# Two passes over the sixth expert tile, with the end of the query stage beside it

## The chip, the cores and the metric

The kernel runs on one core of one Trainium2 chip. The metric is the device time of one execution in microseconds (us); shown are the median of three runs and one profiled execution.

## What is computed

The reference is one step of a streaming trunk of two layers over 640 tokens of width 1024 (512 of a prompt, 8 streams of 16). Each layer mixes tokens (a Mamba-2 scan and an RG-LRU side by side) and then adds the output of retrieved experts. The experts are what the change moves:

```
def peer(h, wq, k1, k2, u, v):                       # per token, 8 heads
    q = (h @ wq).reshape(T, 8, 256)
    s1, s2 = q[..., :128] @ k1.T, q[..., 128:] @ k2.T   # 128 keys each
    v1, i1 = top_k(s1, 16); v2, i2 = top_k(s2, 16)
    sv, si = top_k(v1[..., :, None] + v2[..., None, :], 16)   # of 256 sums
    e = i1[si // 16] * 128 + i2[si % 16]             # 16 experts of 16384
    g = softmax(sv)
    act = gelu(h . u[e]) * g                         # 128 experts a token
    return sum(act * v[e])
...
x = x + g1 * token_mixer(rmsnorm(x) * (1 + sc1) + sh1)
x = x + g2 * peer(rmsnorm(x) * (1 + sc2) + sh2)
```

All of it is fp32. A token takes 128 experts, each a row of u and a row of v (8 KB together), and no two tokens share their choice.

## The kernel before

**Tiles and regions.** The 640 tokens of a layer are five tiles of 128, so there are ten expert tiles, 0 to 9; 0 to 4 are of layer 0. Token mixing and the query stage run over regions: region 0 is tiles 0 to 2 and region 1 is tiles 3 and 4, both of layer 0; regions 2 (tiles 5 to 7) and 3 (tiles 8 and 9) are their like in layer 1. "The sixth tile" is tile 5, the first of layer 1.

**Units and pairs.** An expert tile is 128 units. A unit is one indirect transfer of 128 rows of 8 KB from the table (1.049 MB) into one of the 8 slots of `ring`: four picks of each of the 32 tokens of one block. Two units make a pair, so a tile has 64 pairs, here written (tile, pair). For a pair VectorE multiplies and sums the u halves against `hrow` (`dots`, L1902), ScalarE makes gelu, weight and diagonal of both units (`diagonals`, L1366 to L1376), and TensorE in the next pair multiplies the v halves with the diagonals into PSUM (`values`, L1008) and so frees the two slots; GpSimd (L600) may then start the transfers of the pair four pairs on. `hrow` holds the tokens of one block, turned into rows by TensorE (`turn_h`, L1030) and copied by ScalarE (`h_row`, L1395) in two halves.

**Passes.** A tile in one pass goes through its four blocks once, 32 units each, for all 8 heads. Tile 0 goes in two passes: the four blocks with heads 0 to 3 (16 units each), then the four blocks with heads 4 to 7. Its gathers can therefore start when four heads are chosen. PSUM keeps the sums of the blocks between the passes; `hrow` is changed eight times a tile and not four.

**Steps.** The mixing of a region is a list of numbered steps, in stages: N1 (norm, 12), X (13), S (15 or 19), Z (8), LX (9), LRU (8), M (merge, 33), OUT and the second norm (18), Q (query, 22). A step with a projection takes one 0.524 MB weight tile, loaded by the SP queue (L447) into four slots, four projections ahead. In the Q stage steps Q0 to Q15 project the queries; from Q4 to Q19 VectorE finds the 16 best keys on each side, head by head, for all tiles of the region (`best_keys`), and for the region's first tile also its experts (`sum_up`, `look_up`, `put`) and gates. For the other tiles of a region the experts are chosen later from the kept best keys: a choice of 28 pieces, one per pair (`choice`), at a place given by `choice_at`. When a tile's experts are known VectorE raises `ready`, and the SP queue spreads the picks (`spread`, L533: 16 small transfers from `picked` to `units`), for which GpSimd's first gather of the tile (or of the pass) waits.

**The order.** `plan` writes out by hand one list of entries; an entry is at most one pair and some steps. Every engine walks this list in order. `window(pairs, steps, at, till)` lays steps beside pairs evenly by their weights in `SHARE`, from the pair number `at` to `till`. The plan says which step lies beside which pair; worked out from it:

```
what                                    before               pairs
region 2: N1, X, S                      (3,9)  to (3,30)     22
region 2: Z, LX                         (3,31) to (3,46)     16
region 2: LRU, M                        (3,47) to (4,23)     41
region 2: OUT, second norm              (4,24) to (4,33)     10
region 2: Q0 to Q3                      (4,34) to (4,38)      5
region 2: Q4 to Q13                     (4,39) to (4,51)     13
region 2: Q14 to Q21                    (4,52) to (4,58)      7
choice of tile 6, 28 pieces             (4,59) to (5,23)
region 3: N1, X0 to X9                  (5,9)  to (5,23)     15
region 3: X10 to LX0                    (5,24) to (5,53)     30
region 3: LX1 to LX7                    (5,54) to (5,63)     10
tile 0 and region 0: Q14 to Q21         (0,1)  to (0,15)     15
tile 0 and region 1: N1, X0 to X9       (0,16) to (0,29)     14
tile 0 and region 1: X10 to LX0         (0,30) to (0,58)     29
tile 0 and region 1: LX1 to LX4         (0,59) to (0,63)      5
choice of tile 1, 28 pieces             (0,30) to (0,58)
```

Regions 1 and 3 have the same steps, of the same sizes.

Of the kernel before, what the change touches and what calls it, by code (L numbers as in the profile page):

```python
# [26 lines left out]
BLOCKS = P // BLOCK  # L27
# [85 lines left out]
def around(s, p):  # L113


    if s == TILES_E:
        return BLOCKS * s - 1, None, p
    e, block, quad, place = segment(s, 2 * p)
    i = 2 * p // length(s)
    past = BLOCKS * s + block - 1 if i >= BLOCKS * (passes(s) - 1) and BLOCKS * s + block else None  # L120
    if s == 0 and i == BLOCKS:
        past = None
    after = (s, (block + 1) % BLOCKS) if i + 1 < BLOCKS * passes(s) else (s + 1, 0) if s + 1 < TILES_E else None
    return past, after, place // 2


def plan():
# [22 lines left out]
    def pairs_of(*tiles):  # L150
        return [(s, p) for s in tiles for p in range(PAIRS)]
# [6 lines left out]
    window(first[-14:], [(EARLY, i - BASE[EARLY]["X"]) for i in range(BASE[EARLY]["X"])], 1, 13)  # L158
    window(pairs_of(3, 4), steps_of(2), 9, 122)
    window(pairs_of(5, 6, 7), steps_of(3), 9, 180)  # L160
    window(pairs_of(8), [(REGIONS + t, i) for t in range(3) for i in range(FINAL)], 9, 60)
# [59 lines left out]
def choice_at(t):  # L221


    return PAIRS * (t - 1) + {1: 30, 4: -12, 6: -5}.get(t, 8)

# [9 lines left out]
def passes(s):  # L235
    return 1 if s else 2

# [6 lines left out]
def segment(s, u):  # L244

    i, place = divmod(u, length(s))
    h, block = divmod(i, BLOCKS)
    return (i if s == 0 else 4 * BLOCKS // 2 + BLOCKS * (s - 1) + i), block, h * length(s) + place, place


def spreads(s):

    return BLOCKS * BLOCKS * (s + 2)

# [16 lines left out]
def build(nc, a):  # L271
    ctx = ExitStack()
    with ctx:
# [164 lines left out]
        with nc.Block() as block:  # L438
            @block.sync
            def _(sp):  # L440
# [84 lines left out]
                def spread(s, h):  # L525

                    sp.wait_ge(E["ready"], s + h + 1 if s == 0 else s + 2)
                    if s >= 2:
                        sp.wait_ge(E["wgt"], (s - 1) * UNITS)
                    c = slice(h * length(s), (h + 1) * length(s)) if s == 0 else slice(0, QUADS)  # L530
                    for block in range(BLOCKS):
                        for r in range(BLOCKS):
                            sp.dma_start(units[r * BLOCK:(r + 1) * BLOCK, s % 2, block, :, c],  # L533
                                         picked[block * BLOCK:(block + 1) * BLOCK, s % 2, r, :, c]).then_inc(E["spread"], 16)
# [3 lines left out]
                for e, steps in PLAN:  # L538
                    while n < min(taken + SLOTS, REGIONS * LOADS):
                        next(ahead)  # L540
                    t, place = choice(*e) if e else (None, None)
                    if place == 28:
                        spread(t, 0)
                    for r, i in steps:
                        if r < REGIONS:
                            taken += loads_in(r, i)
                            if r == 0 and i == BASE[0]["Q"] + 13:
                                spread(0, 0)
                            if i == BASE[r]["Q"] + 21:
                                spread(TILE0[r], passes(TILE0[r]) - 1)  # L550
# [4 lines left out]
            def _(pool):  # L555
# [33 lines left out]
                for s in range(TILES_E):  # L589
                    for u in range(UNITS):  # L590
                        if u == 0:
                            pool.wait_ge(E["spread"], 16 * (spreads(s) if s else BLOCKS * BLOCKS))
                        elif s == 0 and u == UNITS // 2:
                            pool.wait_ge(E["spread"], 16 * spreads(0))
                        unit = s * UNITS + u
# [9 lines left out]
            def _(pe):  # L605
# [390 lines left out]
                def values(pair):  # L996
# [3 lines left out]
                    for u in (2 * p, 2 * p + 1):  # L1000
                        unit = s * UNITS + u
                        n = unit % RING
                        e, block, quad, place = segment(s, u)
                        if place == 0 and BLOCKS * s + block >= 2 and (s or quad):
                            pe.wait_ge(E["osb"], BLOCKS * s + block - 1)
# [42 lines left out]
                def pair(s, p):  # L1048
# [3 lines left out]
                    past, after, place = around(s, p)  # L1052
                    if past is not None and place == TURN_OUT[s > 0]:
                        turn_out(past)
                    for half in range(2):
                        if after and place == TURN_H[s > 0][half]:
                            turn_h(*after, half)
# [11 lines left out]
            def _(act):  # L1069
# [328 lines left out]
                def pair(s, p):  # L1398
                    if s < TILES_E:
                        diagonals(s, p)  # L1400
                    past, after, place = around(s, p)
                    if past is not None and place == TAKE_OUT[s > 0]:
                        take_out(past)
                    for half in range(2):
                        if after and place == COPY_H[s > 0][half]:
                            h_row(s, p, half)
# [28 lines left out]
            def _(dve):  # L1435
# [396 lines left out]
                def q_stage(r, i):  # L1832
# [6 lines left out]
                    if 8 <= i < 21 and i % 4 == 0:  # L1839
                        m = (i - 8) // 4  # L1840
                        dve.wait_ge(S["q_ex_out"], at("q_ex_out", r, m))
                        gates(gate_of(s, 2 * m), den[:, 2 * m:2 * m + 2])
                        if m == 3 or r == 0 and m == 1:
                            dve.sem_inc(E["ready"], 1)
# [82 lines left out]
                def pair(s, p):  # L1927
                    if s < TILES_E:
                        dots(s, p)
                    past, _, place = around(s, p)  # L1930
                    if past is not None and place == ADD[s > 0]:
                        residual(past)
# [114 lines left out]
```

## Time and profile before

| | us |
|---|---|
| median of 3 runs (4547.33 to 4551.07) | 4549.44 |
| the profiled execution | 4542.65 |
| its span, first to last instruction | 4540.9 |

The profiled execution lies 1.75 us over its span and 6.79 us under the median of the runs. Of the span TensorE is busy 71%, VectorE 62%, ScalarE 33% and GpSimd 32%; the sixteen DMA engines moved 1610.83 MB, 1342.26 of them in the gathers. A busy share says little here, since every engine walks the same list; what counts is which resource is full in which stretch. GB/s by slice shows where the transfers, which cannot be fewer, are held up. The trace shows pairs by their L1902 instructions: four for a pair, two of them a multiply with sum and two the read of the sum.

### The profile page before, as it was taken

The numbers are of one execution on the slowest core, as the hardware profiler recorded it, in microseconds if no ns is written. First come the engines' busy times: TensorE is split into PE (matmuls) and PEld (weight loads), VectorE is DVE, ScalarE is ACT, GpSimd is POOL, SyncE is SP. The second block draws the span as 40 slices with busy tenths as digits, with TensorE's granted clock in tenths as the row PEclk, the third lists the DMA queues.
The fourth block names the chain that finished last, engine by engine and source line by source line (L and its number), as shares of the span: only waits on it lengthen the run. The fifth ranks groups of instructions, "written<-read, shape, count | busy, mean of one in ns | idle before, by whom it ended". The sixth has DMA issues, their size and how long they took to land. (4 is left out here: it accounts for less than half of the span.)

```text
span 4540.9 us, 60485 instructions
## 1 busy us (share of the span) xinstructions
PE 3202.5 (71%) x22002; PEld 1894.3 (42%) x22002; DVE 2825.0 (62%) x6601; ACT 1484.8 (33%) x4684; POOL 1454.2 (32%) x1298
## 2 busy tenths in 40 slices
PE   7899994777687675489999855776777764444443
PEld 4455552445454442245555423454554442121111
DVE  2422048796864579876744798756854588675454
ACT  2224011543622223354722323534522222232222
POOL 0000003443333343334333323443333334444332
PEclk9999996878898886599999976878888786555555
DMA  8333327999999999989999979999999999999998
GB/s 335 137 146 102 100 81 315 385 373 388 417 417 418 416 405 382 393 340 351 390 386 392 378 283 372 416 387 397 418 418 419 418 411 364 421 419 422 421 421 335
DMA packets 279860, 1610.83 MB, mean 355 GB/s; under 512 B 56410, under 2 KB 61328, under 8 KB 112524
## 3 DMA queue, kind: packets, MB, share of 16 engines
q0 software_dynamic: 184320, 1342.26, 72.4%
q1 hardware_dynamic: 75280, 256.81, 15.1%
q10 hardware_dynamic: 19964, 7.91, 0.6%
q8 instruction: 174, 2.85, 0.3%
q14 instruction: 122, 1.00, 0.1%
HBM read 1597.63 MB, written 7.91 MB: 354 GB/s over the span
## 5 line engine op out<-in xcount | busy, mean ns | idle before, releaser
L600 POOL DMA_INDIRECT ring<-in_peer_uv,units x1280 | 1451.0, 1134 | 3051.8 <-PE psum L1008 2136.4
L1902 DVE SCALAR_TENSOR_TENSOR ring<-ring,hrow 128x1024 f32<-128x1024 f32 x1280 | 1537.6, 1223 | 829.6 <-DMA ring<-in_peer_uv,units 793.9
L1008 PE MATMUL psum<-ring,diag 128*32 128x256 f32 x10240 | 920.3, 491 | 1156.9 <-ACT diag L1376 1153.0
L613 PE MATMUL psum<-hT,wslot 128*128 128x384 f32 (+1 forms) x4224 | 1264.0, 456 | 7.7 <-ACT region L1267 3.1
L1008 PEld LDWEIGHTS psum<-ring,diag 128*32 128x32 f32 x10240 | 320.3, 130 | 1669.5 <-ACT diag L1376 1352.1
L613 PEld LDWEIGHTS psum<-hT,wslot 128*128 128x128 f32 x4224 | 832.6, 201 | 434.3 <-issue 93.4
L1366 ACT ACTIVATE gel<-hid 128x2 f32<-128x2 f32 x640 | 129.1, 202 | 1823.9 <-DVE ring L1902 1767.8
L613 PE MATMUL psum<-region,wslot 128*128 128x384 f32 (+1 forms) x1536 | 458.9, 455 | 3.5 <-ACT region L1267 1.9
L613 PEld LDWEIGHTS psum<-region,wslot 128*128 128x128 f32 x1536 | 302.3, 201 | 154.6 <-issue 31.9
L1376 ACT ACTIVATE diag<-pick,wgt 128x32 f32<-128x32 f32 x1280 | 331.8, 306 | 0.0
L1370 ACT ACTIVATE wgt<-gel,units 128x1 f32<-128x1 f32 x1280 | 307.3, 287 | 20.9
L1522 DVE SCALAR_TENSOR_TENSOR region<-region,vec 128x384 f32<-128x384 f32 (+1 forms) x144 | 80.9, 562 | 182.1 <-ACT region L1142 170.4
L1030 PE MATMUL psum<-ident,hT 128*32 128x128 f32 x2816 | 133.8, 351 | 40.7 <-ACT hrow L1395 30.4
L1030 PEld LDWEIGHTS psum<-ident,hT 128*32 128x32 f32 x2816 | 111.4, 145 | 75.4 <-ACT hrow L1395 28.2
L1280 ACT ACTIVATE region<-psum 128x384 f32<-128x384 f32 (+1 forms) x64 | 27.6, 431 | 305.5 <-PE psum L613 305.5
L1902 DVE DVE_READ_ACCUMULATOR ring<-ring,hrow 128x1 f32 x1280 | 104.7, 82 | 0.0
L1735 DVE SCALAR_TENSOR_TENSOR region<-region,psum 128x384 f32<-128x384 f32 (+1 forms) x32 | 15.5, 486 | 126.3 <-PE psum L613 126.2
L1659 DVE SCALAR_TENSOR_TENSOR region<-region,psum 128x384 f32<-128x384 f32 (+1 forms) x32 | 15.6, 486 | 113.8 <-ACT region L1224 113.7
L1729 DVE SCALAR_TENSOR_TENSOR region<-region,psum 128x384 f32<-128x384 f32 (+1 forms) x32 | 15.5, 485 | 110.2 <-PE psum L613 71.4
L1366 ACT ACT_TABLE_LOAD x65 | 83.4, 1283 | 1.8 <-issue 0.6
L645 PE MATMUL psum<-ring,cT 128*32 128x512 f32 x384 | 47.6, 614 | 31.0 <-DMA ring<-in_w_modt 15.6
L1315 ACT ACTIVATE region<-psum 128x384 f32<-128x384 f32 (+1 forms) x64 | 27.2, 426 | 114.8 <-PE psum L613 114.6
(247 smaller groups left out, 2810.6 us busy)
## 6 DMA issues: line engine op xcount, KB each, us to landing
wslot<-in_w_tiles SPq DMA_DIRECT2D x360, 512.0 KB
ring<-in_w_modt SPq DMA_DIRECT2D x24, 2048.0 KB, 8.9
ring<-in_peer_uv,units POOLq DMA_INDIRECT x1280
wslot<-in_w_gate SPq DMA_DIRECT2D x32, 128.0 KB
region<-in_states_t SPq DMA_DIRECT2D x16, 256.0 KB, 23.3
region<-in_states_n SPq DMA_DIRECT2D x16, 256.0 KB, 8.2
out_new_ssd_sample<-region ACTq DMA_DIRECT2D x16, 256.0 KB, 30.9
xT<-in_x_t SPq DMA_DIRECT2D x1, 2560.0 KB, 8.9
```

What stands on the lines that cost most here:

```text
L600: pool.indirect_dma_start(ring[:, n, :], None, table, bass.IndirectOffsetOnAxis(ap=units[:, s % 2, block, 0, quad:quad + 1].bitcast(U32), ...
L613: last = pe.matmul(out, wslot[:, n % SLOTS, k * P:(k + 1) * P], src(k), start=k == 0, stop=k == KT - 1)
L645: last = pe.matmul(bank(5)[32 * q:32 * q + 32, :], cT[:, 2 * q + kk, :], w, start=kk == 0, stop=kk == 1)
L1008: last = pe.matmul(psum[c * BLOCK:(c + 1) * BLOCK, block % 2, block // 2 * 256:(block // 2 + 1) * 256], diag[:, n, :], ring[:, n, D + c * ...
L1030: last = pe.matmul(out[c * BLOCK:(c + 1) * BLOCK, :], v, ident[:], start=True, stop=True)
L1280: act.activation(lay.gates[:, q, :], bank(3 + 2 * q)[:, 0:lay.N], ACT.Tanh, scale=0.5).then_inc(S["mg"], 1)
L1315: act.activation(lay.qT[:, j % 2, q, :], bank(3 + q)[:, 0:lay.N], ACT.Copy).then_inc(S["q_taken"], 1)
L1366: act.activation(gel[:, v], hid[:, v], ACT.Gelu_apprx_tanh).then_inc(E["gelu"], 1)
L1370: act.activation(wgt[:, c:c + 1], gel[:, c:c + 1], ACT.Copy, scale=units[:, s % 2, block, 1, quad + u:quad + u + 1])\
L1376: act.activation(diag[:, pick % RING, :], pick32[:], ACT.Copy, scale=wgt[:, pick % 16:pick % 16 + 1])\
L1522: st(dve.scalar_tensor_tensor(y, x[:, k:k + NY], w(k), y, ALU.mult, ALU.add))
L1902: dve.scalar_tensor_tensor(out=ring[:, n, 0:D], in0=ring[:, n, 0:D], scalar=1.0, in1=hrow[:, e % 2, :], op0=ALU.mult, op1=ALU.mult, accum_ ...
```

## The change

Tile 5 goes in two passes, as tile 0 does (`passes`), and the functions that had tile 0 written into them (`segment`, `spreads`, `around`, `spread`, the waits of GpSimd and TensorE, the places of the hand-overs in a block of 8 pairs) go by `passes(s)`. The plan's two windows from tile 3 to tile 7 become three: region 2 up to Q13 beside the first 124 pairs of tiles 3 and 4, its last eight steps Q14 to Q21 beside 16 pairs (four of tile 4, twelve of tile 5), and region 3 from pair 12 of tile 5 on. The choice of tile 6, which needs the best keys of all eight heads, moves from pair -5 to pair 30 of tile 5 (`choice_at`).

```
what                                    after                pairs
region 2: N1, X, S                      (3,9)  to (3,32)     24
region 2: Z, LX                         (3,33) to (3,49)     17
region 2: LRU, M                        (3,50) to (4,29)     44
region 2: OUT, second norm              (4,30) to (4,40)     11
region 2: Q0 to Q3                      (4,41) to (4,45)      5
region 2: Q4 to Q13                     (4,46) to (4,60)     15
region 2: Q14 to Q21                    (4,61) to (5,11)     15
region 3: N1, X0 to X9                  (5,12) to (5,26)     15
region 3: X10 to LX0                    (5,27) to (5,56)     30
region 3: LX1 to LX5                    (5,57) to (5,63)      7
choice of tile 6, 28 pieces             (5,30) to (5,58)
```

Region 3 ends beside the same pair of tile 7 as before. The spread of tile 5's first four heads lies at Q13, pair (4,59), and that of the other four at Q21, pair (5,9).

```diff
--- before.py
+++ after.py
@@ -117,9 +117,7 @@
         return BLOCKS * s - 1, None, p
     e, block, quad, place = segment(s, 2 * p)
     i = 2 * p // length(s)
-    past = BLOCKS * s + block - 1 if i >= BLOCKS * (passes(s) - 1) and BLOCKS * s + block else None
-    if s == 0 and i == BLOCKS:
-        past = None
+    past = BLOCKS * s + block - 1 if i > BLOCKS * (passes(s) - 1) or s and i == 0 else None
     after = (s, (block + 1) % BLOCKS) if i + 1 < BLOCKS * passes(s) else (s + 1, 0) if s + 1 < TILES_E else None
     return past, after, place // 2
 
@@ -156,8 +154,10 @@
     first = fresh + pairs_of(1, 2)
     window(first[:-14], steps_of(1), 0, 64 - 28 + 125)
     window(first[-14:], [(EARLY, i - BASE[EARLY]["X"]) for i in range(BASE[EARLY]["X"])], 1, 13)
-    window(pairs_of(3, 4), steps_of(2), 9, 122)
-    window(pairs_of(5, 6, 7), steps_of(3), 9, 180)
+    half = BASE[2]["Q"] + 14
+    window(pairs_of(3, 4)[:124], steps_of(2)[:half], 9, 124)
+    window(pairs_of(3, 4)[124:] + pairs_of(5)[:12], steps_of(2)[half:], 0, 14)
+    window(pairs_of(5)[12:] + pairs_of(6, 7), steps_of(3), 0, 168)
     window(pairs_of(8), [(REGIONS + t, i) for t in range(3) for i in range(FINAL)], 9, 60)
     window(pairs_of(9), [(REGIONS + 3, i) for i in range(FINAL)], 9, 60)
     for p in range(9):
@@ -221,7 +221,7 @@
 def choice_at(t):
 
 
-    return PAIRS * (t - 1) + {1: 30, 4: -12, 6: -5}.get(t, 8)
+    return PAIRS * (t - 1) + {1: 30, 4: -12, 6: 30}.get(t, 8)
 
 
 def choice(s, p):
@@ -233,7 +233,8 @@
 
 
 def passes(s):
-    return 1 if s else 2
+
+    return 2 if s in (0, 5) else 1
 
 
 def length(s):
@@ -245,12 +246,12 @@
 
     i, place = divmod(u, length(s))
     h, block = divmod(i, BLOCKS)
-    return (i if s == 0 else 4 * BLOCKS // 2 + BLOCKS * (s - 1) + i), block, h * length(s) + place, place
+    return BLOCKS * sum(passes(t) for t in range(s)) + i, block, h * length(s) + place, place
 
 
 def spreads(s):
 
-    return BLOCKS * BLOCKS * (s + 2)
+    return BLOCKS * BLOCKS * sum(passes(t) for t in range(s + 1))
 
 
 def state_loads(l, i):
@@ -524,10 +525,10 @@
 
                 def spread(s, h):
 
-                    sp.wait_ge(E["ready"], s + h + 1 if s == 0 else s + 2)
+                    sp.wait_ge(E["ready"], sum(passes(t) for t in range(s)) + h + 1)
                     if s >= 2:
                         sp.wait_ge(E["wgt"], (s - 1) * UNITS)
-                    c = slice(h * length(s), (h + 1) * length(s)) if s == 0 else slice(0, QUADS)
+                    c = slice(h * length(s), (h + 1) * length(s))
                     for block in range(BLOCKS):
                         for r in range(BLOCKS):
                             sp.dma_start(units[r * BLOCK:(r + 1) * BLOCK, s % 2, block, :, c],
@@ -544,8 +545,8 @@
                     for r, i in steps:
                         if r < REGIONS:
                             taken += loads_in(r, i)
-                            if r == 0 and i == BASE[0]["Q"] + 13:
-                                spread(0, 0)
+                            if passes(TILE0[r]) == 2 and i == BASE[r]["Q"] + 13:
+                                spread(TILE0[r], 0)
                             if i == BASE[r]["Q"] + 21:
                                 spread(TILE0[r], passes(TILE0[r]) - 1)
                 for _ in ahead:
@@ -589,9 +590,9 @@
                 for s in range(TILES_E):
                     for u in range(UNITS):
                         if u == 0:
-                            pool.wait_ge(E["spread"], 16 * (spreads(s) if s else BLOCKS * BLOCKS))
-                        elif s == 0 and u == UNITS // 2:
-                            pool.wait_ge(E["spread"], 16 * spreads(0))
+                            pool.wait_ge(E["spread"], 16 * (spreads(s) - BLOCKS * BLOCKS * (passes(s) - 1)))
+                        elif passes(s) == 2 and u == UNITS // 2:
+                            pool.wait_ge(E["spread"], 16 * spreads(s))
                         unit = s * UNITS + u
                         n = unit % RING
                         _, block, quad, _ = segment(s, u)
@@ -1001,7 +1002,7 @@
                         unit = s * UNITS + u
                         n = unit % RING
                         e, block, quad, place = segment(s, u)
-                        if place == 0 and BLOCKS * s + block >= 2 and (s or quad):
+                        if place == 0 and BLOCKS * s + block >= 2 and (quad or block < 2 or passes(s) == 1):
                             pe.wait_ge(E["osb"], BLOCKS * s + block - 1)
                         pe.wait_ge(E["diag"], unit + 1)
                         for c in range(BLOCKS):
@@ -1050,10 +1051,10 @@
                     if 0 <= n < TILES_E * PAIRS:
                         values(n)
                     past, after, place = around(s, p)
-                    if past is not None and place == TURN_OUT[s > 0]:
+                    if past is not None and place == TURN_OUT[passes(s) == 1]:
                         turn_out(past)
                     for half in range(2):
-                        if after and place == TURN_H[s > 0][half]:
+                        if after and place == TURN_H[passes(s) == 1][half]:
                             turn_h(*after, half)
 
                 pe.wait_ge(consts, CONSTS)
@@ -1399,10 +1400,10 @@
                     if s < TILES_E:
                         diagonals(s, p)
                     past, after, place = around(s, p)
-                    if past is not None and place == TAKE_OUT[s > 0]:
+                    if past is not None and place == TAKE_OUT[passes(s) == 1]:
                         take_out(past)
                     for half in range(2):
-                        if after and place == COPY_H[s > 0][half]:
+                        if after and place == COPY_H[passes(s) == 1][half]:
                             h_row(s, p, half)
                     t, place = choice(s, p)
                     if place == 26:
@@ -1840,7 +1841,7 @@
                         m = (i - 8) // 4
                         dve.wait_ge(S["q_ex_out"], at("q_ex_out", r, m))
                         gates(gate_of(s, 2 * m), den[:, 2 * m:2 * m + 2])
-                        if m == 3 or r == 0 and m == 1:
+                        if m == 3 or passes(s) == 2 and m == 1:
                             dve.sem_inc(E["ready"], 1)
                     if 4 <= i < 20:
                         j = (i - 4) // 2
@@ -1928,7 +1929,7 @@
                     if s < TILES_E:
                         dots(s, p)
                     past, _, place = around(s, p)
-                    if past is not None and place == ADD[s > 0]:
+                    if past is not None and place == ADD[passes(s) == 1]:
                         residual(past)
                     t, place = choice(s, p)
                     if t and place < 24:
```

## Rows read from the trace of the kernel before

**Rows 1.** The page's 40 slices: clock granted to TensorE, transfer rate

```profile
PEclk9999996878898886599999976878888786555555
GB/s 335 137 146 102 100 81 315 385 373 388 417 417 418 416 405 382 393 340 351 390 386 392 378 283 372 416 387 397 418 418 419 418 411 364 421 419 422 421 421 335
```

**Rows 2.** Windows, region 2 beside tiles 3 and 4; busy us by engine

```profile
core 0: us, PE busy (x) PEld busy (x) DVE busy (x) ACT busy (x) POOL busy (x), PEclk, DMA share, GB/s
1909.70:2250.50 340.80, 313.14 (x1906) 174.84 (x1906) 238.74 (x419) 186.19 (x449) 122.50 (x96) 0.94 0.90 351
2250.50:2460.00 209.50, 207.44 (x1116) 111.81 (x1114) 92.84 (x165) 55.74 (x197) 75.80 (x61) 1.00 0.98 391
2460.00:2529.20 69.20, 61.94 (x384) 33.13 (x384) 34.76 (x59) 22.28 (x68) 25.32 (x23) 0.96 0.98 386
2529.20:2554.10 24.90, 23.03 (x121) 12.12 (x118) 12.91 (x24) 9.01 (x33) 9.49 (x8) 0.90 0.97 374
2554.10:2659.60 105.50, 85.62 (x518) 50.20 (x516) 96.41 (x371) 24.29 (x78) 28.37 (x29) 0.92 0.92 353
2659.60:2724.70 65.10, 26.76 (x202) 14.56 (x202) 61.07 (x236) 15.45 (x46) 13.78 (x14) 0.68 0.70 253
```

**Rows 3.** Waits from 2554.1 to 2724.7 us: us, times, longest

```profile
POOL ring L600 <- PE psum L1008: 112.1, 21, 9.8
ACT gel L1366 <- DVE ring L1902: 67.9, 18, 13.1
```

**Rows 4.** Windows, same columns: choice of tile 6, region 3, tile 6

```profile
2724.70:2793.50 68.80, 31.50 (x310) 12.75 (x310) 59.96 (x146) 17.98 (x79) 30.18 (x29) 0.57 0.93 374
2793.50:2883.30 89.80, 70.16 (x463) 49.61 (x462) 78.85 (x185) 47.42 (x180) 31.25 (x30) 0.81 0.97 393
2883.30:3072.20 188.90, 134.36 (x1233) 82.26 (x1231) 117.89 (x191) 70.46 (x213) 80.54 (x60) 0.80 1.00 399
3072.20:3135.30 63.10, 44.35 (x356) 30.10 (x356) 40.24 (x81) 26.22 (x113) 24.03 (x21) 0.85 0.97 379
3135.30:3513.70 378.40, 273.13 (x1995) 185.45 (x1994) 236.43 (x522) 141.91 (x435) 144.85 (x128) 0.85 1.02 418
```

**Rows 5.** Windows, same columns: tile 0 from its second pair, tile 1

```profile
716.30:804.00 87.70, 47.91 (x439) 25.25 (x432) 78.96 (x264) 25.50 (x89) 32.32 (x29) 0.70 0.93 380
804.00:889.60 85.60, 67.18 (x537) 48.44 (x529) 60.04 (x130) 44.22 (x173) 33.95 (x30) 0.88 0.98 392
889.60:1078.50 188.90, 134.24 (x1284) 83.39 (x1281) 157.22 (x321) 72.61 (x215) 76.07 (x58) 0.78 0.97 386
1078.50:1117.80 39.30, 28.51 (x233) 20.80 (x231) 20.64 (x42) 15.39 (x59) 10.95 (x10) 0.85 0.94 352
1117.80:1497.00 379.20, 276.58 (x2039) 188.38 (x2042) 243.68 (x541) 147.52 (x460) 139.17 (x128) 0.85 1.02 418
```

**Rows 6.** Timeline of VectorE around pair (4,46), beside which no step lies

```profile
2615.95 1.23 DVE L1902 SCALAR_TENSOR_TENSOR ring<-ring,hrow 128x1024 f32<-128x1024 f32 x1
...
2618.25 1.22 DVE L1902 SCALAR_TENSOR_TENSOR ring<-ring,hrow 128x1024 f32<-128x1024 f32 x1
```

**Rows 7.** Windows of L1902 alone: four instructions are a pair

```profile
2724.70:2793.50 68.80, 33.71 (x59) 0.57 0.93 374
```

**Rows 8.** Groups of TensorE in the merge stage, 2250.5 to 2460.0 us

```profile
L613 PE MATMUL psum<-hT,wslot 128*128 128x384 f32 x260 | 88.1, 492 | 0.0
...
L1008 PE MATMUL psum<-ring,diag 128*32 128x256 f32 x496 | 33.2, 385 | 1.9 <-ACT diag L1376 1.8
```

**Rows 9.** Timelines of the SP queue at the spreads of tiles 0 and 5

```profile
692.03 10.33 SPq L533 DMA_DIRECT2D units<-picked  x16
...
796.95 10.92 SPq L533 DMA_DIRECT2D units<-picked  x16
...
2722.38 11.30 SPq L533 DMA_DIRECT2D units<-picked  x16
```

**Rows 10.** Waits of the SP queue from 889.6 to 1078.5 us

```profile
SPq L533 <- DVEq L1953: 5.4, 1, 5.4
```

## The prediction

> **What bounds the kernel now.** I first read the 40 slices, 113.5 us each, for the transfer rate. It stands at 416 to 422 GB/s where nothing but gathers and a few weights run, and falls below that in three places after the gathers have begun [rows 1]. Bytes can't be saved (the change moves the same picks and weights), so 418 GB/s, the rate of tiles 1 and 6 [rows 4, 5], is the floor, and the question is how much time the transfers are held up. At 418 GB/s a pair (2.097 MB) is 5.02 us and a weight tile (0.524 MB) 1.25 us.
>
> Then I cut the stretch from pair (3,9) to the end of tile 6 at the borders of the plan's stages, by counting four L1902 instructions to a pair as in [rows 7] (59 for 14 pairs; some records are missing), and read the windows. Time lost against the floor is a window's length times (1 - rate/418). N1 to LRU of region 2 lose 54.6 us, M 13.5, OUT 5.3, Q0 to Q3 2.6, Q4 to Q13 16.4 and Q14 to Q21 25.7 [rows 2]; the first half of tile 6's choice 7.2, region 3 beside tile 5 5.4 + 8.6 + 5.9, tile 6 nothing [rows 4]. That is 145 us in all.
>
> The reader is to see that the cause changes on the way. Up to OUT TensorE is the full one: busy 207.4 of 209.5 us in M at a granted clock of 1.00, while VectorE is busy 92.8. In Q4 to Q21 it is VectorE: 96.4 of 105.5 and 61.1 of 65.1 us, while TensorE falls to 26.8 of 65.1 us and the rate to 253 GB/s [rows 2]. The chain of that stretch stands in the waits: ScalarE's gelu waits 67.9 us for VectorE's products, so diagonals and freed slots come late, and GpSimd waits 112.1 of 170.6 us before it may start the next gather [rows 3]. There VectorE's picking of keys sets the time, and each pair that is laid beside it gets its gathers almost free: pair (4,46), with no step beside it, passes in 2.30 us, the two products alone [rows 6], against 5.02 us of transfer.
>
> **The change part by part.** It removes no work and adds little. It moves pairs: counting from the two tables of the plan, N1 to LRU get 4 pairs more (48 to 52), M 2, OUT 1, Q4 to Q13 2, Q14 to Q21 8 (7 to 15); the 14 pairs with the first half of tile 6's choice vanish as a stretch of their own, and region 3 beside tile 5 has 3 fewer (55 to 52). The sum is zero, as it must be.
>
> *Seven pairs into N1 to OUT.* Here TensorE's projections set the time. A projection instruction of 384 columns takes 88.1/260 = 0.34 us, sixteen a step, 5.4 us; the eight small products of a unit, two units a pair, take 33.2/496 x 16 = 1.07 us [rows 8]. So an added pair costs no less than its 2.30 us on VectorE [rows 6] in order, and no more than 5.02 us of transfer: 16.1 to 35.1 us for seven. The idle transfer time there (54.6, 13.5, 5.3) exceeds what each of the three stretches gets (20.1, 10.0, 5.0), so I take a value near the low end: +18.
>
> *Two pairs into Q4 to Q13.* VectorE-bound, 2.30 us each: +4.6 (up to 10.0).
>
> *Eight pairs into Q14 to Q21.* The trace holds this very stretch once: tile 0 has Q14 to Q21 of region 0, with as many tiles in the region, beside 15 pairs in two passes, and takes 87.7 us at 380 GB/s [rows 5]. Before, it is 65.1 us: +22.6. By eight bare pairs it would be +18.4, with all eight at transfer speed +40.2. Tile 0 includes what two passes add: twice the hand-overs of `hrow` and a second spread.
>
> *The 14 pairs of the choice.* Their stretch is gone: -68.8 [rows 4].
>
> *Region 3 beside tile 5.* Before, 55 pairs from N1 on take 89.8 + 188.9 + 63.1 = 341.8 us [rows 4]. After, 52 pairs hold the steps up to LX5 and all 28 pieces of the choice, with S and Z. Again tile 0 has it: region 1 from N1 to LX4 with the 28 pieces of tile 1 beside X10 to LX0, 48 pairs in 85.6 + 188.9 + 39.3 = 313.8 us [rows 5]. Four more pairs are 9.2 to 20.1 us; most here run at transfer speed, so 16. One more weight tile is 1.3. That is 331.1: -10.7 (-17.5 to -6.6).
>
> *Tiles 6 and 7.* Two steps (LX6, LX7) are owed at the end of tile 5, 2.5 us of weights at most. Tile 1, which also begins that much behind, takes 379.2 us against tile 6's 378.4 [rows 4, 5]. I take +2. From tile 8 on nothing changes.
>
> *The queues.* SP gets one batch of spreads more, and its pieces are half as long. A half batch takes 10.33 and 10.92 us to issue, a full one 11.30 [rows 9], so +10 us on SP. Weights queued behind it are those of region 3, four ahead and not due while Q14 to Q21 run, which cost nothing; without that cover it is +10. The spread of tile 6 moves from X9 to LX2 and can hold SP while it waits for VectorE, 5.4 us in tile 0 [rows 10]; LX3's weights are loaded ahead, and tile 0's window has the same wait inside. "DMA: Bandwidth & Descriptors" of the Trainium skill (Specifications) puts line rate at pieces of 512 B and more, which speaks against pieces of 64 B in place of 128; the rows show that SP's issue sets the price and not the size, so by rule or by row nothing is added.
>
> Sum: 18 + 4.6 + 22.6 - 68.8 - 10.7 + 2 = -32.3 us. The profiled execution of 4542.65 us (span 4540.9 and 1.75 around it) becomes 4510.4; the median of the runs lies 6.79 above it, so 4517.
>
> **The rivals.**
>
> *The seven pairs are not hidden* (chance 0.15). Region 2 loses time in stalls as well as on TensorE, and an added pair's transfer may fall outside them: +35 in place of +18, a sum of -15, 4534 us. For it speaks the M stage at 391 GB/s, only 7% under the floor [rows 2]; against it the 54.6 us lost before M.
>
> *The first gather of tile 5 comes late* (0.06). `ready` comes with Q12 beside (4,57); the spread then takes 10.3 us to issue plus its landing, and GpSimd wants the picks once (4,60) is through, after three pairs at 2.3 and Q13's part of VectorE, some 13 us. The ring holds eight landed units in this stretch, so the loss stays under 10 us: 4527.
>
> *The choice beside S and Z makes it slower* (0.09). Fourteen pieces cost VectorE 59.96 - 33.71 = 26.3 us [rows 4, 7], so 28 cost 52.5. In S and Z each step waits for VectorE's part of an earlier one. If all 52.5 us land on region 3's own pace (188.9 us for X10 to LX0 without a piece [rows 4]), that stretch is 241 and not 193, and the sum is +16: 4565. It ends slower once over 41 of the 52.5 us show. For it: VectorE would be busy 117.9 + 52.5 of 188.9 us, 90%. Against it: tile 0 does the same steps with 28 pieces, at VectorE 157.2 busy, in the same 188.9 us with one pair less [rows 4, 5].
>
> *Transfers are at their limit anyway* (0.04). If the mean rate over the kernel were the limit, spreading pairs would move nothing: 4549, no change. For it: 1610.83 MB over the span are a mean of 355 GB/s. Against it: tile 6 holds 418 for 378 us [rows 4], and the slices reach 422 [rows 1]. "DMA: Bandwidth & Descriptors" of the Trainium skill (Specifications) gives a limit of about 358 GB/s from HBM for one core; by that rule this rival would hold. The trace disagrees by 60 GB/s; the Trainium skill's page adds that single-core runs reach 425.
>
> **How the numbers follow.** The forecast itself has 0.66, with its own bounds: 16.1 + 4.6 + 18.4 - 68.8 - 17.5 = -47, to about -16, where half of what the first rival adds is left open. The range reaches from about -50, a little under the sum of the low bounds, to -5, the sum of the high ones with tile 0's row kept for Q14 to Q21 (35.1 + 10.0 + 22.6 - 68.8 - 6.6 + 2.5): 4499 to 4544. About 9 us (0.2%) is what a measurement tells from no change. Faster: 0.66, two thirds of the first rival and of the late gather, 0.80. Same: the rest of these two, the limit and a touch of the choice, 0.12. Slower: 0.08.
>
> **What would show it.** Right: the window from Q14 to Q21 runs at about 380 GB/s and lasts near 88 us; pair (5,12) starts near 2770 us (1909.7 + 619.5 + 18 + 24.9 + 110.1 + 87.7; pair (5,9) starts at 2793.5 before) and tile 6 near 3101 (before 3135.3); slice 24, the one from 2611 us on (283 GB/s), rises above 340. The first rival shows as N1 to OUT lasting over 650 us; the late gather as GpSimd waiting for `units<-picked` a second time; the choice as VectorE over 90% busy and a rate under 370 GB/s beside S and Z. The prediction would be wrong above all if tile 0's rows, taken with region 0 and 1, do not carry over to tile 5.

## The result and the profile after

The changed kernel takes 4518.92 us (median of 4 runs, 4512.28 to 4523.05) against 4548.39 for the kernel before in the same set: a ratio of 0.9936, 95% interval 0.9924 to 0.9949. A second set, beside other kernels, gave 4520.79 us and 0.9946 (0.9932 to 0.996). The forecast was 4517. The profiled execution took 4512.28 us, 30.4 less than the one of before.

The transfer rate of the changed kernel by slice answers to [rows 1]:

```profile
GB/s 333 135 155 98 103 80 303 382 374 407 418 418 419 419 404 383 418 321 363 397 411 405 409 334 362 403 365 394 418 417 419 418 403 367 421 420 422 421 421 330
```

The slice that stood at 283 GB/s stands at 334, and five of the six before it are higher too; the three behind it (372, 416 and 387 before) are lower. The windows below go by the stages of the plan after: N1 to LRU, M, OUT, Q0 to Q3, Q4 to Q13, Q14 to Q21 with the two bare pairs behind it (pairs with no step beside them), region 3 in three parts beside tile 5, and tile 6. They answer to [rows 2] and [rows 4].

```profile
1903.60:2254.50 350.90, 323.43 (x2006) 179.10 (x2006) 248.39 (x436) 188.28 (x468) 130.04 (x104) 0.92 0.91 361
2254.50:2469.00 214.50, 211.59 (x1185) 113.91 (x1187) 97.77 (x174) 58.39 (x208) 83.89 (x65) 0.99 1.01 408
2469.00:2537.10 68.10, 61.18 (x362) 32.35 (x354) 39.04 (x66) 22.73 (x72) 27.16 (x24) 0.98 1.01 418
2537.10:2563.30 26.20, 25.45 (x158) 13.23 (x148) 12.08 (x21) 8.72 (x31) 9.70 (x8) 0.85 0.95 371
2563.30:2676.40 113.10, 88.08 (x537) 51.00 (x530) 101.88 (x384) 27.03 (x92) 33.23 (x30) 0.89 0.90 348
2676.40:2764.70 88.30, 42.04 (x385) 21.94 (x388) 79.92 (x268) 25.17 (x88) 30.36 (x29) 0.68 0.89 352
2764.70:2854.80 90.10, 75.34 (x579) 52.96 (x572) 62.84 (x136) 46.77 (x185) 39.65 (x33) 0.84 0.98 396
2854.80:3055.50 200.70, 139.77 (x1365) 87.01 (x1363) 159.16 (x322) 72.61 (x216) 69.15 (x60) 0.79 0.96 380
3055.50:3101.30 45.80, 34.39 (x258) 24.22 (x262) 29.14 (x60) 23.23 (x87) 12.77 (x12) 0.80 0.93 359
3101.30:3481.30 380.00, 272.87 (x2038) 185.88 (x2032) 241.08 (x533) 145.18 (x451) 152.80 (x130) 0.86 1.02 418
```

The reader is to see two things. M and OUT went from 391 and 386 GB/s to 408 and 418: three more pairs were put there, and the two stretches together became 3.9 us longer (282.6 for 278.7) where three pairs' transfers at the floor are 15 us. The granted clock did not bring this: it is 0.99 and 0.98 in the two, after 1.00 and 0.96 [rows 2]. And the query stage is still VectorE's: busy 79.9 of 88.3 us in Q14 to Q21, at 352 GB/s. Its ScalarE and GpSimd still wait as in [rows 3], but over 201 us and 30 pairs, no longer over 171 and 20 (waits from 2563.3 to 2764.7 us):

```profile
POOL ring L601 <- PE psum L1009: 130.6, 28, 12.4
ACT gel L1367 <- DVE ring L1903: 106.0, 24, 12.6
```

One number serves for all that follows: the time from pair (3,9), where the two plans part, to the first pair of tile 8, where they have met again. It was 1967.7 us before (1909.7 to 3877.4) and is 1942.1 (1903.6 to 3845.7) in the first profile of the changed kernel, 1937.0 in the second.

### The profile page after: what moved, and what is told of

Same layout as the page of the kernel before. It is cut to its first block and busy times, and to the rows that moved or that the text cites. A ratio compares the mean times of both kernels' runs of the same rounds, so it can differ in the third digit from the quotient of the medians.

```text
span 4510.5 us, 61035 instructions
## 1 busy us (share of the span) xinstructions
PE 3210.7 (71%) x22258; PEld 1901.3 (42%) x22258; DVE 2827.8 (63%) x6601; ACT 1486.8 (33%) x4690; POOL 1458.4 (32%) x1298
## 5 line engine op out<-in xcount | busy, mean ns | idle before, releaser
L1031 PE MATMUL psum<-ident,hT 128*32 128x128 f32 x3072 | 148.3, 352 | 73.6 <-ACT hrow L1396 55.9
L1031 PEld LDWEIGHTS psum<-ident,hT 128*32 128x32 f32 x3072 | 122.0, 145 | 112.5 <-issue 63.1
L1281 ACT ACTIVATE region<-psum 128x384 f32<-128x384 f32 (+1 forms) x64 | 27.6, 432 | 307.1 <-PE psum L614 307.0
L1104 ACT ACTIVATE region<-psum 128x512 f32<-128x512 f32 x24 | 14.3, 597 | 153.7 <-PE psum L654 141.8
```

The costliest lines, as they stand in the source:

```text
L1031: last = pe.matmul(out[c * BLOCK:(c + 1) * BLOCK, :], v, ident[:], start=True, stop=True)
L1281: act.activation(lay.gates[:, q, :], bank(3 + 2 * q)[:, 0:lay.N], ACT.Tanh, scale=0.5).then_inc(S["mg"], 1)
```

## Experiments

Ratios are to the kernel before, run on the same chip, with 95% intervals. "The stretch" is from (3,9) to tile 8, in each one's profile.

**1. The two passes alone.** Everything of the change but the windows and the choice's place. The two lines added at the end make the SP queue wait until the first spread of tile 5 has landed before it issues the second.

```diff
-    half = BASE[2]["Q"] + 14
...
+    window(pairs_of(3, 4), steps_of(2), 9, 122)
+    window(pairs_of(5, 6, 7), steps_of(3), 9, 180)
...
-    return PAIRS * (t - 1) + {1: 30, 4: -12, 6: 30}.get(t, 8)
+    return PAIRS * (t - 1) + {1: 30, 4: -12, 6: -5}.get(t, 8)
...
+                    if s and h:
+                        sp.wait_ge(E["spread"], 16 * (spreads(s) - BLOCKS * BLOCKS))
```

> Tile 5 goes in two passes, but the plan and the place of tile 6's choice stay as before (the SP queue also waits for the first spread before it issues the second). Theory A (the gain is in where pairs lie: beside steps that VectorE or TensorE sets a pair costs 2.0 to 2.3 us, in a stretch at the transfer rate 5): the passes alone bring nothing and cost four more hand-overs and half a spread, which lie under transfers: within 5 us of before, 4545 to 4555. Theory B (the gain comes from gathers of tile 5 that may start early): 4517 to 4535. Theory C (the hand-overs every 8 pairs cost, and the change won in spite of them): over 4555.

Measured: 4552.25 us, ratio 1.0014 (1.0001 to 1.0026); the stretch takes 1966.9 us, 0.8 less than before. Of the 6 us between the medians none is in the stretch, so the passes by themselves bring nothing and cost next to nothing. Theory A's range held, and theories B and C fall. One part did move: region 3's N1 to X9, with the pieces of the choice beside them, took 102.6 us where it took 89.8 [rows 4]; other parts of the stretch were shorter.

```profile
2803.00:2905.60 102.60, 77.03 (x560) 55.16 (x557) 78.32 (x184) 48.00 (x181) 33.52 (x30) 0.79 0.93 368
```

**2. More pairs beside the query stage, without the rest.** The kernel before with heavier weights for Q4 to Q17 of region 2.

```diff
+    if r == 2 and BASE[r]["Q"] + 4 <= i < BASE[r]["Q"] + 18:
+        return 35
     return SHARE[max((BASE[r][name], name) for name in SHARE if BASE[r][name] <= i)[1]]
```

> The kernel before with one pass, but the weights of Q4 to Q17 in region 2 raised from 24 to 35 (6 for none of them): Q4 to Q21 get 6 pairs more (26 in place of 20), all taken from N1 to OUT. Theory A: N1 to OUT loses 6 pairs at the 2.0 us that an added pair cost there in the changed kernel (-12), Q4 to Q21 gains 6 at 2.3 (+14): +2, 4545 to 4555, no change. Theory D (what pays is to relieve the stretch in which VectorE is full, wherever the pairs come from): 6 pairs at 5 us out, at 2.3 in: -16, 4533.

Measured: 4551.83 us, ratio 1.0009 (0.9998 to 1.002); the stretch 1967.5 us. Its windows are N1 to OUT (83 pairs, 89 before), Q4 to Q13 (17 pairs, 13 before) and Q14 to Q21 (8 pairs; 6 before, 62.8 us, without the bare pair of 2.3 us that [rows 2] has in its 65.1):

```profile
1914.20:2520.90 606.70, 572.89 (x3308) 316.59 (x3307) 352.15 (x616) 254.90 (x680) 207.71 (x167) 0.97 0.92 356
2545.50:2663.10 117.60, 91.89 (x597) 53.01 (x596) 106.66 (x392) 28.82 (x99) 38.82 (x36) 0.90 0.96 377
2663.10:2730.60 67.50, 31.74 (x234) 17.13 (x234) 63.47 (x242) 16.96 (x56) 21.11 (x19) 0.70 0.86 328
```

The transfers of the query stage are much better fed (377 and 328 GB/s for 353 and 253), and nothing is won: the query stage is 16.8 us longer for its six pairs (185.1 for 105.5 + 62.8), 2.8 each, and N1 to OUT is 12.8 us shorter for its six, 2.1 each, and sank to 356 GB/s (369 over the same stages before). A high rate in one stage is no gain where the pairs come out of another stage in which they were as cheap. Theory D falls.

**3. The choice at pair 12 and not 30.**

```diff
-    return PAIRS * (t - 1) + {1: 30, 4: -12, 6: 30}.get(t, 8)
+    return PAIRS * (t - 1) + {1: 30, 4: -12, 6: 12}.get(t, 8)
```

> The changed kernel with the choice of tile 6 at pair 12 of tile 5 and not 30, so its 28 pieces lie beside N1, X and the first steps of S. Theory E (the 11.9 us that X10 to LX0 got longer are the pieces beside S and Z): that stretch falls from 200.7 to 189 to 194 us, N1 to X9 rises by at most 3: 4509 to 4515. Theory F (it is the variation of the stalls there, not the pieces): X10 to LX0 stays at 195 to 205, total 4515 to 4523.

Measured: 4527.19 us, ratio 0.9954 (0.9937 to 0.9971); the stretch 1944.7 us.

```profile
2773.60:2883.00 109.40, 79.07 (x600) 54.94 (x592) 90.55 (x227) 47.70 (x189) 39.49 (x35) 0.80 0.91 359
2883.00:3071.80 188.80, 136.92 (x1358) 85.67 (x1358) 130.58 (x236) 72.79 (x215) 75.10 (x60) 0.78 0.97 374
```

X10 to LX0 fell from 200.7 to 188.8 us as theory E expected, but N1 to X9 rose from 90.1 to 109.4, where at most 3 were expected. The sum of the two is 7.4 us worse, and the total lies above the ranges of both theories. The place at pair 30 looks the better one: the stretch is 3 to 8 us shorter with it in the two profiles of the changed kernel (1942.1 and 1937.0), though the intervals of the ratios overlap. It would be so for a reason that the forecast did not have.

**4. Without the pieces.** Left out are the 24 working pieces of tile 6's choice, so that tile 6 gathers by the picks that tile 4 left behind.

```diff
-                    if t and place < 24:
+                    if t and t != 6 and place < 24:
```

> The changed kernel without the 24 working pieces of tile 6's choice; left out is the choice of tile 6's experts, so tile 6 gathers rows of picks that tile 4 left in the buffer. It prices the choice where it now lies. Theory E: X10 to LX0 falls by 8 to 15 us, 4504 to 4511. Theory F: by under 4 us, 4515 to 4523. Were all 52 us of VectorE's work on the path, 4467.

Measured: 4503.52 us, ratio 0.9905 (0.9886 to 0.9924); the stretch 1922.2 us, 14.8 to 19.9 less than in the two profiles of the changed kernel. X10 to LX0:

```profile
2862.50:3048.10 185.60, 134.70 (x1361) 84.63 (x1360) 118.66 (x194) 74.51 (x219) 75.40 (x59) 0.81 1.00 398
```

That is 185.6 against 200.7 and 195.3: VectorE has 40 us less to do there (118.7 for 159.2), and leaving them out shortens it by 10 to 15. Theory E holds, with a total just under its 4504 to 4511, and the rival of the forecast in which over 41 us would show is refuted by size.

**5. The changed kernel again.**

> The changed kernel once more, for the spread between executions and beside the next three on one chip. The 6 us by which its first profile was ahead at pair (3,9), before anything that the change touches, should be chance: (3,9) between 1900 and 1915 us; total 4512 to 4524, ratio to before 0.993 to 0.995.

Measured: 4520.79 us, ratio 0.9946 (0.9932 to 0.996). Its pair (3,9) starts at 1907.4 us, after 1903.6 in the first profile. In the thirteen profiles of this study it starts between 1903.6 and 1919.1 us, though no plan differs before it: that is how far executions differ by chance, and six of the 30 us between the first two profiles are of this kind.

**6. A narrow second window.** Four pairs of tile 5 in place of twelve (and the wait of experiment 1).

```diff
-    window(pairs_of(3, 4)[124:] + pairs_of(5)[:12], steps_of(2)[half:], 0, 14)
-    window(pairs_of(5)[12:] + pairs_of(6, 7), steps_of(3), 0, 168)
+    window(pairs_of(3, 4)[124:] + pairs_of(5)[:4], steps_of(2)[half:], 0, 6)
+    window(pairs_of(5)[4:] + pairs_of(6, 7), steps_of(3), 0, 176)
```

> The changed kernel with the second window over 4 pairs of tile 5 and not 12: Q14 to Q21 beside 7 pairs or so in place of 15, region 3 from pair (5,4). Theory A: eight pairs go from a stretch where one costs 2.3 us to stretches at 380 to 418 GB/s where one costs 4 to 5: +14 to +22 on the changed kernel, 4532 to 4541. Theory B (the early gathers and the choice's new place are what pays): within 4 us of the changed kernel, 4515 to 4523.

Measured: 4518.96 us, ratio 0.9944 (0.9929 to 0.9959); the stretch 1937.7 us: no loss, where 14 to 22 us were expected. Its windows are Q14 to Q21 with two bare pairs (8 pairs, from (4,60)), then region 3 to the end of tile 5:

```profile
2684.00:2751.20 67.20, 29.05 (x197) 16.26 (x199) 62.63 (x235) 15.56 (x46) 14.14 (x14) 0.70 0.69 254
2751.20:3112.30 361.10, 267.00 (x2443) 175.94 (x2436) 277.78 (x567) 158.45 (x548) 153.21 (x122) 0.83 0.99 398
```

Eight pairs (60 for 52) cost 361.1 - 336.6 = 24.5 us beside region 3, 3.1 each and not 4 to 5 (3.5 by the second profile of the changed kernel, 332.8 us), and region 3 also got further by them. The seven fewer beside Q14 to Q21 saved 88.3 - 67.2 = 21.1, 3.0 each, and the eighth came out of Q4 to Q13 (110.8 us for 113.1). The prices are nearly equal, so the width does not matter here. This order has one wait that the changed kernel has not: GpSimd stands 10.3 us for tile 6's picks; what it costs was not taken apart. Theory A had the right kind of price and the wrong one for region 3; theory B's number came true without its reason, which experiments 1 and 10 exclude.

**7. A wide second window.** The same with 24 pairs of tile 5 and 156 for region 3, in two sets.

```diff
+    window(pairs_of(3, 4)[124:] + pairs_of(5)[:24], steps_of(2)[half:], 0, 26)
+    window(pairs_of(5)[24:] + pairs_of(6, 7), steps_of(3), 0, 156)
```

> The second window over 24 pairs of tile 5: Q14 to Q21 beside 27 pairs, region 3 from (5,24), so that the 28 pieces lie beside N1, X and S. Theory A: Q14 to Q21 reaches the transfer floor (27 pairs, 136 to 140 us), so most of the 12 pairs cost 4 to 5 us there too and what region 3 gives back is 12 pairs at about the same: -6 to +2, 4512 to 4521. Theory D (relieving VectorE pays on): -26, 4493. From the run with the choice at 12 a further cost is seen: pieces beside N1 and X cost up to 19 us, which would put it at 4525 to 4540.

> The kernel with the second window over 24 pairs of tile 5 once more, with more rounds, against the changed kernel's ratio of 0.9936 and 0.9946: if its first 0.9928 was no chance, 0.992 to 0.994 again and a profile of 1930 to 1937 us from (3,9) to (8,0) (1942.1 and 1937.0 in the two profiles of the changed kernel).

Measured: 4509.86 us, ratio 0.9928 (0.9911 to 0.9945), and 4510.08 us, ratio 0.9917 (0.9903 to 0.993); the stretch 1934.2 and 1934.5 us. It is the fastest full version found, 11 us ahead of the changed kernel by the medians of one set (4509.86 and 4520.79) and under theory A's range of 4512 to 4521. How much of this is real is less sure: the second interval overlaps the changed kernel's first (0.9924 to 0.9949) and ends just under its second (0.9932 to 0.996), and the stretches differ by only 3 to 8 us. In the second profile Q14 to Q21 with two bare pairs is 26 pairs in

```profile
2687.90:2827.70 139.80, 65.85 (x695) 33.49 (x686) 106.67 (x314) 39.89 (x152) 62.90 (x55) 0.67 0.97 397
```

that is 5.4 us a pair at 397 GB/s: the stage has reached the transfers' side and took the 136 to 140 us that theory A expected, and theory D's -26 did not come. N1 to X9 took 99.7 us for 14 pairs (90.1 for 15 in the changed kernel), part of the feared cost; it is made up elsewhere.

**8. The same change for tile 8 too.**

```diff
+    half = BASE[3]["Q"] + 14
+    window(pairs_of(5)[12:] + pairs_of(6, 7)[:124], steps_of(3)[:half], 0, 176)
+    window(pairs_of(7)[60:] + pairs_of(8)[:12], steps_of(3)[half:], 0, 14)
+    window(pairs_of(8)[12:], [(REGIONS + t, i) for t in range(3) for i in range(FINAL)], 0, 48)
...
-    return PAIRS * (t - 1) + {1: 30, 4: -12, 6: 30}.get(t, 8)
+    return PAIRS * (t - 1) + {1: 30, 4: -12, 6: 30, 9: 30}.get(t, 8)
...
-    return 2 if s in (0, 5) else 1
+    return 2 if s in (0, 5, 8) else 1
```

> The same change once more for tile 8: two passes, region 3 up to Q13 beside pairs up to (7,59), its Q14 to Q21 beside 16 pairs of tiles 7 and 8, the choice of tile 9 at pair 30 of tile 8, the final steps from pair 12 of tile 8. Theory A: 12 pairs without a step at the end of tile 7 and 10 more at the start of tile 8, all at the floor of 5.0 us, move beside region 3's steps, where VectorE or TensorE sets the time in part (X10 to LX0 at 380 GB/s, the query stage in tile 7 at about 365); they can save what region 3 still loses against the floor, 47 us by the windows, at most; 15 to 25 on the changed kernel, 4494 to 4504. Theory B or D: as little as the two-tile region's VectorE load, which is a third lighter, allows: under 5 us, 4514 to 4519.

Measured: 4516.37 us, ratio 0.9932 (0.9919 to 0.9945), 3 to 4 us ahead of the changed kernel by the medians, which the intervals don't tell from nothing, where theory A expected 15 to 25. The number lies in the range given for theories B and D (4514 to 4519), whose reasons experiments 1 and 2 had refuted; whether the lighter query stage of two tiles plays a part was not tested. From region 3's start to tile 8, and tile 8:

```profile
2778.30:3851.90 1073.60, 728.83 (x5946) 484.12 (x5942) 718.39 (x1605) 381.69 (x1308) 422.88 (x363) 0.82 0.99 402
3851.90:4184.60 332.70, 156.06 (x1656) 81.48 (x1652) 241.69 (x567) 103.07 (x369) 141.64 (x128) 0.61 1.00 411
```

The first is 2.6 to 7.4 us shorter than in the changed kernel (1081.0 and 1076.2), the second 8.6 longer (324.1). From pair (3,9) to the end of tile 8 it takes 2266.8 us, against 2266.2 and 2262.1 in the two profiles of the changed kernel. Tile 8 ran at 421 GB/s in the changed kernel, so it had little idle transfer time to give; what region 3 gave back was less than the 47 us by which its windows lie over the floor had let me think. Why so little of these 47 us can be had stays open.

**9. The choice's place alone.** The kernel before, with the choice at pair 30.

```diff
-    return PAIRS * (t - 1) + {1: 30, 4: -12, 6: -5}.get(t, 8)
+    return PAIRS * (t - 1) + {1: 30, 4: -12, 6: 30}.get(t, 8)
```

> The kernel before, one pass and its old windows, with the choice of tile 6 alone moved to pair 30 of tile 5. Theory G (what pays is that the 14 pairs with nothing but the choice beside them, at the transfer floor of 5.0 us, are filled with or replaced by steps; the choice's own place costs): those pairs stay at 4.8 to 5.0 us each without their pieces, and the pieces cost 8 to 15 us beside X10 to LX0, less 0 to 5 beside N1 and X: +3 to +12, 4548 to 4557. Theory H (the move of the choice is itself part of the gain): 4535 to 4543.

Measured: 4554.53 us, ratio 1.0017 (1.0007 to 1.0027); the stretch 1973.7 us, 6.0 more than before. The pairs without a step, and X10 on (31 pairs, 191.9 us before):

```profile
2723.50:2793.80 70.30, 28.86 (x298) 11.98 (x302) 37.29 (x64) 17.98 (x79) 31.22 (x28) 0.56 0.89 358
2884.40:3091.00 206.60, 138.05 (x1226) 82.66 (x1217) 160.98 (x323) 70.70 (x214) 79.04 (x61) 0.77 0.97 383
```

With VectorE busy 37.3 of 70.3 us the bare pairs (15 here, from (4,58)) still take 4.7 each; GpSimd waits 5.9 us for tile 5's picks at their start, and from 2753.0 us on the rate is 422 GB/s. So in that stretch of the kernel before the choice had been free, and the pairs had been dear. Moved, the pieces cost 14.7 us from X10 on, the size of experiment 4, but the eleven pairs behind, (5,55) to (6,1), are 10.1 us shorter than before (60.2 for 70.3), and 6.0 us are left over the whole stretch. Theory G holds, H falls.

**10. All of it with one pass.** Region 2 laid up to Q21 beside (4,62), region 3 from (5,7), the choice at pair 30.

```diff
-    window(pairs_of(3, 4), steps_of(2), 9, 122)
-    window(pairs_of(5, 6, 7), steps_of(3), 9, 180)
+    window(pairs_of(3, 4), steps_of(2), 9, 127)
+    window(pairs_of(5, 6, 7), steps_of(3), 7, 180)
```

> As much of the change as one pass allows: region 2 laid up to pair (4,62), with Q21 there, region 3 from (5,7), as soon as tile 4's sums are back in x, the choice at pair 30. Seven pairs fewer are bare. Theory G with the late gather: seven pairs at 5.0 us become pairs at 2.3 (-19), the pieces cost +3 to +12, and GpSimd, which wants tile 5's picks after (4,60), waits some 20 to 27 us for Q21 and the spread, of which 10 to 15 reach the end: 4540 to 4553. Theory I (a second pass isn't needed, only the plan): no such wait reaches the end, 4520 to 4532.

Measured: 4549.38 us, ratio 1.0007 (0.9998 to 1.0016); the stretch 1973.4 us. GpSimd's timeline where tile 5 begins, and the windows of Q14 to Q21 and of the eight pairs behind it:

```profile
2750.32 0.94 POOL L600 DMA_INDIRECT ring<-in_peer_uv,units  x1 [44.83 <-DMA units<-picked]
```

```profile
2674.40:2738.70 64.30, 28.81 (x216) 15.49 (x204) 60.31 (x232) 14.64 (x45) 9.38 (x10) 0.68 0.51 190
2738.70:2792.40 53.70, 14.40 (x118) 4.75 (x122) 20.52 (x35) 9.73 (x43) 21.00 (x20) 0.50 0.77 310
```

GpSimd stands 44.8 us for the picks, the rate falls to 190 GB/s, and the eight pairs take 6.7 us each. The total came as theory G said, the wait about twice as long as its 20 to 27 us. This is what the two passes are for: they bring no time themselves, but with one pass this filling of the plan won nothing. Another order with one pass was not tried.

## Why the prediction was right, point by point

- **Seven pairs into N1 to OUT, +18.** Measured 10.1 + 5.0 - 1.1 = +14.0, 2.0 a pair. That lies under my low bound of 16.1, for which I had taken VectorE's 2.30 us for two products in order as the least that a pair can cost. VectorE is not full there, so its own time was no bound: in M and OUT its waits for projections at `xT` (L1748, L1749 after) fell from 31.7 to 14.8 us with three pairs more. Experiment 2 gives 2.1 on taking six out. The rival of 5.02 us each did not occur.
- **Q0 to Q3, 0, and two pairs into Q4 to Q13, +4.6.** +1.3 and +7.6. That is 3.8 a pair in Q4 to Q13 and not 2.30, so this term was too small by 3 us although VectorE is as busy there as I said (101.9 of 113.1 us).
- **Eight pairs into Q14 to Q21, +22.6 by tile 0's row.** 88.3 us for 65.1 [rows 2]: +23.2. Tile 0's 87.7 [rows 5] carried over to half a microsecond, though the rate is 352 GB/s and not the 380 that I named as the sign.
- **The stretch of the choice, -68.8.** Gone. Experiment 9 shows why it was dear: its pairs take 4.7 to 5 us with or without the pieces.
- **Region 3 beside tile 5, -10.7.** 336.6 us for 341.8, -5.2; in the second profile 332.8, -9.0. Here tile 0's row was a little too kind: X10 to LX0 took 200.7 and 195.3 us for 30 pairs, tile 0's 188.9 for 29. Experiments 4 and 9 put the pieces at 10 to 15 us there, against the 52.5 of the slower rival.
- **Tiles 6 and 7, +2.** 744.4 us for 742.1: +2.3.

The sum of the measured terms is -25.6 in the first profile and -30.7 in the second, against -32.3; most of what is left of the first profile's 30.4 lies before (3,9) and is chance. The medians fell by 29.5 us in the first set and by 23.6 in the second. So the mechanism held and its size was somewhat too kind, by 5.5 us in region 3 above all. That the total came within 2 us of 4517 is in part luck: the terms' errors partly cancel (-4 in N1 to OUT against +3 and +5.5), and against the second set, with its 23.6 us, the forecast of 32.3 misses by 9. **The late gather** did not occur: no GpSimd wait for `units<-picked` falls near tile 5, the only long ones being in tile 0. Experiment 10 shows what one looks like. **The limit at the mean rate** fell with M at 408 and OUT at 418 GB/s. The slice that I said would rise above 340 rose to 334. Pair (5,12) started at 2764.7 and 2768.2 us (2770 said) and tile 6 at 3101.3 and 3101.0 (3101 said), from a (3,9) that came 6.1 and 2.3 us earlier than the sum assumed.

What the prediction had only in part is the rule behind its own sum. It said that a pair beside VectorE's picking "gets its gathers almost free". Experiment 2 shows that VectorE's stretch is not special: in the stages measured a pair costs 2.0 to 3.8 us beside steps that another engine sets, and 5 where transfers do. The gain is the 14 pairs of the choice at 4.9 us, and three more from region 3's stretch, spent again at 2.0 to 3.8 us, less the price of pieces that had been hidden: 10 to 15 us beside X10 to LX0, and over the whole stretch 6.0 us by moving them (experiment 9) or 15 to 20 by leaving them out (experiment 4). Experiment 8 does not fit this rule as it stands, since bare pairs moved beside region 3 brought next to nothing there.

Open: why the pieces beside N1 and X cost 19 us in experiment 3 and 13 in experiment 1, both with two passes, and nothing with one (89.8 us with pieces before, 90.6 without in experiment 9). The hand-overs of `hrow` every eight pairs are the difference, but no run here took them apart.

## What to carry to other kernels

Where all engines walk one list, price a piece of work by the stretch in which it lies and not by its own length: look for a stretch that stands at the transfer floor with little beside it, and for stretches held by another engine, and move work between the two kinds. A better rate in one stage says nothing until the stage that gave the work up is looked at. A restructuring such as the second pass may bring no time and still be what makes the better order possible, so try the order and the means apart.

## Not expected

The stretch up to pair (3,9), the same in every plan here, took 1193 to 1208 us from the first gather's products in the profiles, while the stretch of some 1940 us behind it repeated within about 5 us in the two kernels that were profiled twice; in these profiles most of the spread between executions came from the part ahead of it. And the width of the second window hardly mattered from 4 to 24 pairs of tile 5 (1937.7, 1942.1 and 1937.0, 1934.2 and 1934.5 us for the stretch).
